# Reordering a mixer's output work and halving a Fourier product in a one-core Trainium2 layer

## The chip, the cores and the metric

One core of a Trainium2 chip runs one launch of the kernel. The metric is the device time of that launch in microseconds (us), as the median of several runs. A profile is one execution recorded by the hardware profiler; its span runs from the first to the last instruction. The engines are PE (TensorE, matrix products, with PEld for its weight loads), DVE (VectorE), ACT (ScalarE), POOL (GpSimd, which also issues some DMAs here) and SP (SyncE, which issues the weight DMAs). Each engine executes its own queue in order and waits on semaphores for the others.

## The reference

One layer of a diffusion backbone over 256 latent tokens with a prefix of 256 context tokens, 2048 channels, float32. Cut to what matters:

```
x, ctx = half SwiGLU FFN with norms, shift, scale, gate     (d_ff 5632, tokens 512)
q, k, v, beta, g, z, f = mixer_inputs(pre(x or ctx))        (one projection w_in, short conv)
o = gated delta rule, both directions, chunks of 64, 8 heads of 128, ctx state then latents
gd = rmsnorm(o, g_onorm) * silu(z)
ff = f.reshape(b, l, 8, 128)
fr = fft2(ff, axes=(positions, channels), norm='ortho').real
x  = post(x, concat([gd, fr]) @ w_out)
x  = half SwiGLU FFN again                                  (latent tokens only)
post(x, y): x + weight * mod_gate * rmsnorm(y, g_post)
```

The Fourier part of one group is real(W_t f W_c). With f real, it is cos_t (f cos_c) - sin_t (f sin_c), where cos_t and sin_t are 256 x 256 over positions. The cosine is symmetric and the sine antisymmetric under n -> 256 - n.

## The kernel before

All engines run hand-ordered queues; semaphores (`hs[...]` counts per head, from table `PER`) tie them. Weights stream through four raw slots by SP; ACT writes the high half of each and DVE the low half (`split_hi`, `split_lo`), and PE makes three products for each pair, so that float32 accuracy comes out of a faster format.

Stages in order of time: modulation rows and the first gate products; 11 FFN rounds over 512 tokens, in whose shadow DVE accumulates modulation rows (`mac`) that PE folds (`mod_reduce`, `transpose_mod`); norms; 20 pairs of projection tiles (`PROJ`) with convolution and gates; the mixer; the output projection; norms; 11 FFN rounds over 256 tokens; the end.

The mixer (`mixer_pe`, `mixer_dve`, `mixer_act`) runs one loop of ten passes, i from -1 to 8. A pass works on three heads at once: `a` is head i+1 (its chunk matrices are prepared), `m` is head i (its triangular systems are solved in five levels `y_level`/`x_level` on PE with `level_Y`, `level_S`, `level_T` on DVE; its Fourier group goes through `fnet_channels`, `fnet_mid`, `fnet_positions`, `fnet_out`, `fnet_hi`, `fnet_lo`), and `b` is head i-1 (its scan of eight steps `scan_read`, `scan_u`, `scan_write`, `scan_state`). `was` is head i-2: its normed and gated output (`out_root` and `out_hi` on ACT, `output` and `output_lo` on DVE) is written in this pass. Text below calls the pass with i = n "head n".

PE's order in a pass: `decay_sums(a)`, `products_k(a)`, `scan_write(b, 0)`, `y_level(m, 0)`, `scan_read(b, 1)`, `token_k(m, 0)`, `x_level(m, 0)`, and so on through five levels, with `fnet_positions(m)` after the fifth `x_level`, then `solve_w`, `out_sums(b)` and `solve_v`. DVE's order at the start of a pass: `chunk_half(a)`, `scan_state(b, 0)`, `chunk_matrix(a)`, `output(was)`, `output_lo(was)`, `level_Y(m, 0)`, `scan_u(b, 1)`, two `token_k`, `level_S(m, 0)`. PE's `x_level(m, 0)` waits for `level_Y(m, 0)`. POOL makes `strict_b` for a head as soon as the `n_mat` of the one before it is done.

`fnet_positions` sums four products into bank `B_B`, each of 128x128 weights from `f_mid` and 256 columns from the constants `dft_t` (cosine and sine, two halves of positions). In float32 one such product is two PE instructions. DVE copies the result to `f_out`, ACT writes its high part and DVE its low part to `xn2`.

The gains of the post norms lie across partitions in `post_g` (128 x 16) and are needed as rows on every partition. `gain_out` on POOL writes them element by element to DRAM (`gain_rows`, four rows: gain 0 for context, and gains 0, 1 and 2 for the latents), and `gain_in` reads a row back as a broadcast of 1 MB. The coefficients come from `coefs(r)` on DVE.

## Time and profile before

| | |
|---|---|
| three timed runs | 3143.86, 3140.58, 3143.63 us, median 3143.63 |
| profiled execution | 3139.69 us, span 3137.9 us |
| mean granted PE clock | 0.983 of 2.4 GHz |
| PE busy | 3018.2 us, 96% of the span |
| DVE, ACT, POOL busy | 1801.8, 965.7, 22.6 us |
| mixer, 1945 to 2265 us | PE busy 295.0 of 320 us |

Busy time is the time in which an engine has an instruction under way. Durations of PE instructions overlap (the end of a matmul is modelled), so for PE the distance from the start of one group to the start of the next is read. A bracket behind an instruction in a timeline gives the idle time of its engine before it and whose instruction ended it.

### The profile page before, as it was taken

What the parts mean: (1) busy time and instruction counts of PE and PEld (TensorE: products, weight loads), DVE (VectorE), ACT (ScalarE), POOL (GpSimd) and SP (SyncE); (2) the same over time, 40 slices, a digit from 0 to 9 for tenths busy, and PEclk for the clock granted to TensorE, in tenths of its full rate; (3) what the DMA queues carried; (4) which work ended last, traced back from release to release, by engine and by line L of the source; (5) the groups of instructions that cost most, each with busy time, mean ns of one, the idle gap of its engine ahead of it and who ended that gap; (6) DMA issues with size and microseconds to landing.
All of it is one profiled execution on the core that took longest, in us unless ns stands there. A gap on an engine that the chain in (4) does not pass through costs nothing. (4 is left out here: it accounts for less than half of the span.)

```text
span 3137.9 us, 44120 instructions
## 1 busy us (share of the span) xinstructions
PE 3018.2 (96%) x18262; PEld 2492.7 (79%) x18262; DVE 1801.8 (57%) x1977; ACT 965.7 (31%) x1211; POOL 22.6 (1%) x27
## 2 busy tenths in 40 slices
PE   5899999999999999998979999999998999999998
PEld 3588888888888888887868898777777888888887
DVE  3337565675555656555665464666655665565666
ACT  3222222222212122221343345222234433343433
POOL 0000000000000000000000000000000000000000
PEclk9999999999999999999989999999999999999999
DMA  8835444454544657567723353000154555555554
GB/s 316 294 104 189 146 162 148 152 196 136 171 151 148 247 189 274 198 217 177 287 63 94 108 164 105 2 2 2 64 171 143 183 192 187 187 183 191 182 193 135
DMA packets 305077, 506.05 MB, mean 161 GB/s; under 512 B 8253, under 2 KB 227909, under 8 KB 289061
## 3 DMA queue, kind: packets, MB, share of 16 engines
q1 hardware_dynamic: 302624, 494.73, 47.3%
q0 software_dynamic: 1472, 8.85, 0.8%
q8 instruction: 117, 1.92, 0.3%
q10 hardware_dynamic: 836, 0.33, 0.0%
q14 instruction: 28, 0.22, 0.0%
HBM read 501.75 MB, written 2.13 MB: 161 GB/s over the span
## 5 line engine op out<-in xcount | busy, mean ns | idle before, releaser
L1959 PE MATMUL ps<-xn,parts 128*128 128x512 f32 (+1 forms) x9008 | 1796.2, 361 | 16.4 <-DVE parts L1311 13.8
L1959 PEld LDWEIGHTS ps<-xn,parts 128*128 128x128 f32 x9008 | 1521.5, 189 | 290.1 <-issue 18.3
L1311 DVE TENSOR_TENSOR parts<-raw,parts 128x1024 fp32r<-128x1024 f32 x642 | 767.7, 1221 | 448.8 <-ACT parts L751 448.5
L751 ACT ACTIVATE parts<-raw 128x1024 fp32r<-128x1024 f32 x642 | 664.1, 1055 | 1114.6 <-PE ps L1959 889.6
L1959 PE MATMUL ps<-parts,h_parts 128*128 128x512 f32 x3168 | 729.5, 390 | 1.6 <-DVE h_f L1339 1.5
L1959 PEld LDWEIGHTS ps<-parts,h_parts 128*128 128x128 f32 x3168 | 591.5, 188 | 135.2 <-issue 6.1
L1327 DVE SCALAR_TENSOR_TENSOR macc<-raw,cs,macc 128x2048 f32<-128x2048 f32 x150 | 348.1, 2346 | 0.0
L1421 DVE TENSOR_TENSOR acc<-acc,ps 128x512 f32<-128x512 f32 x160 | 110.0, 687 | 212.4 <-PE ps L1959 212.4
L774 ACT ACTIVATE h_parts<-h_f 128x512 fp32r<-128x512 f32 (+1 forms) x42 | 35.1, 837 | 351.6 <-DVE h_f L1386 351.6
L1386 DVE TENSOR_TENSOR h_f<-silu_g,ps 128x1024 f32<-128x1024 f32 x20 | 24.4, 1222 | 140.5 <-PE ps L1959 140.5
L1959 PE MATMUL ps<-parts,xn 128*128 128x512 f32 x384 | 91.7, 394 | 0.0
L1959 PEld LDWEIGHTS ps<-parts,xn 128*128 128x128 f32 x384 | 71.0, 188 | 15.1 <-issue 0.5
L1413 DVE TENSOR_TENSOR acc<-acc,ps 128x1024 f32<-128x1024 f32 x44 | 53.7, 1221 | 39.1 <-PE ps L1959 36.1
L1380 DVE TENSOR_REDUCE h_f<-ps 128x512 f32<-128x1024 f32 x22 | 27.0, 1226 | 73.3 <-PE ps L1959 73.3
L1374 DVE TENSOR_REDUCE silu_g<-ps 128x512 f32<-128x1024 f32 x22 | 27.0, 1226 | 72.3 <-PE ps L1959 72.3
L1599 DVE SCALAR_TENSOR_TENSOR cv<-ps,convT,cv 128x248 f32<-128x248 f32 (+3 forms) x160 | 66.1, 471 | 0.0
L1681 PE MATMUL ps<-g_S,g_Y 64*64 64x64 f32 x1280 | 48.6, 228 | 14.6 <-DVE g_Y L1101 13.8
L1388 DVE TENSOR_TENSOR h_parts<-h_f,h_parts 128x512 fp32r<-128x512 f32 (+1 forms) x42 | 39.8, 946 | 37.9 <-ACT h_parts L774 37.9
L1681 PEld LDWEIGHTS ps<-g_S,g_Y 64*64 64x64 f32 x1280 | 43.1, 142 | 20.2 <-DVE g_Y L1101 16.4
L1959 PE MATMUL ps<-raw,cpad 128*32 128x512 f32 x256 | 40.7, 722 | 15.4 <-DMA raw<-in_w_mod 14.0
L1681 PE MATMUL ps<-g_T,n_T 64*64 64x64 f32 x1280 | 48.4, 228 | 2.3 <-DVE g_T L1107 2.1
L1681 PEld LDWEIGHTS ps<-g_T,n_T 64*64 64x64 f32 x1280 | 42.8, 141 | 7.9 <-DVE g_T L1107 3.8
(220 smaller groups left out, 1257.1 us busy)
## 6 DMA issues: line engine op xcount, KB each, us to landing
raw<-in_w_mod SPq DMA_DIRECT2D x144, 1024.0 KB, 5.4
raw<-in_w_gate SPq DMA_DIRECT2D x88, 1024.0 KB, 5.1
raw<-in_w_up SPq DMA_DIRECT2D x88, 1024.0 KB, 5.1
raw<-in_w_down SPq DMA_DIRECT2D x88, 1024.0 KB, 5.1
raw<-in_w_in SPq DMA_DIRECT2D x41, 1024.0 KB, 5.3
raw<-in_w_out SPq DMA_DIRECT2D x16, 1024.0 KB, 5.1
gr<-gain_rows POOLq DMA_DIRECT2D x3, 1024.0 KB, 7.6
x_in<-in_ctx SPq DMA_DIRECT2D x2, 1024.0 KB, 6.8
```

Of the source, the lines that this page charges most:

```text
L751: nc.scalar.activation(parts[:, unit % PART_SLOTS, 0, :], raw[:, slot, b * UNIT:(b + 1) * UNIT], ACT.Copy).then_inc(hi_ready, 1)
L774: nc.scalar.activation(gpart[:, 0, 2 * s:2 * s + 2, :], h_f32[:, :, 0:N], ACT.Copy).then_inc(h_hi, 1)
L1311: nc.vector.tensor_tensor(parts[:, pslot, 1, :], raw[:, slot, b * UNIT:(b + 1) * UNIT], parts[:, pslot, 0, :].bitcast(F32), ALU.subtract)\
L1327: ins = nc.vector.scalar_tensor_tensor(macc[:, s, :], raw[:, slot, :], cs[:, k, s:s + 1], macc[:, s, :], ALU.mult, ALU.add)
L1374: nc.vector.tensor_reduce(silu_g[:, :, 0:N], halves(4 * s), axis=mybir.AxisListType.X, op=ALU.add).then_inc(g_sum, 1)
L1380: nc.vector.tensor_reduce(h_f32[:, :, 0:N], halves(up), axis=mybir.AxisListType.X, op=ALU.add).then_inc(u_sum, 1)
L1388: nc.vector.tensor_tensor(gpart[:, 1, 2 * s:2 * s + 2, :], h_f32[:, :, 0:N], gpart[:, 0, 2 * s:2 * s + 2, :].bitcast(F32), ALU.subtract)\
L1413: nc.vector.tensor_tensor(a[:, :, cols], a[:, :, cols], ps[:, bank:bank + 2, :], ALU.add).then_inc(down_added, 1)
L1421: nc.vector.tensor_tensor(a[:, t, cols], a[:, t, cols], ps[:, down_bank(tiles, j, t), :], ALU.add).then_inc(down_added, 1)
L1599: nc.vector.scalar_tensor_tensor(o, s_, tap, o, ALU.mult, ALU.add).then_inc(conv_op, 1)
L1681: return nc.tensor.matmul(o, lhsT, rhs, start=start, stop=stop)
L1959: return nc.tensor.matmul(o, lhsT, rhs, start=start, stop=stop)
```

## The change

The post gains: `post_g` now holds two vectors at a time side by side; PE transposes them to 32 x 128 (`post_rows`), ACT copies them to `row_sb` (`post_row`), and POOL writes each pair with one DMA of 32 runs of 512 bytes. The second pair (gains 1 and 2 of the latents) is made right after the first norms. `coefs` becomes `post_coefs` and `pre_coefs`.

The mixer: `output` becomes `output_root` and `output_gate`. DVE runs `level_Y(m, 0)` and `scan_u(b, 1)` first, then `output_root`; `output_gate` comes after `scan_state(b, 3)` and `output_lo` after `scan_u(b, 5)`. ACT's `out_hi` moves from behind `out_root` to behind `transposed`. The last pass keeps its order.

The Fourier positions: cosine and sine products go to separate halves of bank `B_B` and are made for positions 0 to 128 alone, 129 columns. ACT copies the cosine sum to `f_mid` (`fnet_even`); DVE adds the sine sum for positions 0 to 128, and subtracts it, both read in reverse, for 129 to 255. `fnet_mid` waits for DVE's reads of the head before.

```diff
         cs = sb("cs", [P, KT, 2], R_LATE + 2048)
+        row_sb = sb("row_sb", [32, P], R_LATE + 2304)
         pick = sb("pick", [P, 2, 32], R_LATE + 3072)
...
         row_out, gr_ok = sem("row_out"), sem("gr_ok")
+        post_ok, row_T, row_ok = sem("post_ok"), sem("row_T"), sem("row_ok")
         coef_ok, y_scaled, ln_ok, acc3_zero = sem("coef_ok"), sem("y_scaled"), sem("ln_ok"), sem("acc3_zero")
...
             "kT": 2, "kd_ok": 2, "kbg_ok": 2, "vT": 2, "vb_ok": 8, "gam_mm": 1, "gam_exp": 1, "qg_ok": 1, "dT_mm": 1,
-            "dT_exp": 1, "qk_mm": 1, "p_half": 1, "p_ok": 3, "f_a": 1, "f_mid_ok": 1, "f_b": 1, "f_v": 1, "f_hi": 1,
+            "dT_exp": 1, "qk_mm": 1, "p_half": 1, "p_ok": 3, "f_a": 1, "f_mid_ok": 1, "f_b": 1, "f_even": 1, "f_v": 2, "f_hi": 1,
             "f_lo": 1,
...
-            def gain_out(n, s, coefs_done):
-
-                pool.wait_ge(coef_ok, coefs_done)
-                pool.dma_start(gain_rows[n].rearrange("(k p) -> p k", p=P), post_g[:, s, :],
-                               allow_slow_non_contiguous=True).then_inc(row_out, 16)
+            def gain_out(pair):
+
+                pool.wait_ge(row_ok, pair + 1)
+                pool.dma_start(gain_rows[2 * pair:2 * pair + 2].rearrange("n (k p) -> (n k) p", p=P), row_sb[:])\
+                    .then_inc(row_out, 16)
...
-                pool.wait_ge(row_out, 16 * max(2, n + 1))
+                pool.wait_ge(row_out, 16 * (n // 2 + 1))
                 pool.dma_start(dst, gain_rows[n:n + 1, :].to_broadcast([P, D])).then_inc(gr_ok, 16)
-            gain_out(0, 0, 4)
-            gain_out(1, 1, 4)
+            gain_out(0)
             pool.wait_ge(units_done, PART_SLOTS + 2 * S_KV.weight - 8)
...
+            gain_out(1)
             pool.wait_ge(mod_ok, 16)
...
                 strict_beta(Head(pool, h))
-            gain_out(2, 1, 6)
             pool.wait_ge(hs["qk_mm"], HEADS)
...
             nc.gpsimd.memset(acc3[:], 0.0).then_inc(acc3_zero, 1)
-            gain_out(3, 1, 7)
             gain_in(3, gr[:, 0, :])
...
                 m.wait("f_a")
-                m.last("f_b")
+                m.last("f_v")
                 nc.scalar.activation(flat(f_mid[:]), ps[:, B_A, :], ACT.Copy).then_inc(hs["f_mid_ok"], 1)
+
+            def fnet_even(m):
+                m.wait("f_b")
+                nc.scalar.activation(f_mid[:, 0, 0:P + 1], ps[:, B_B, 0:P + 1], ACT.Copy).then_inc(hs["f_even"], 1)
...
                     out_root(was)
-                    out_hi(was)
                 if m:
...
                     transposed(a)
+                if was:
+                    out_hi(was)
                 if m:
...
                 if m:
+                    fnet_even(m)
                     fnet_hi(m)
...
+
+            def post_row(pair):
+
+                act.wait_ge(row_T, pair + 1)
+                if pair:
+                    act.wait_ge(row_out, 16 * pair)
+                nc.scalar.activation(row_sb[:], ps[0:32, 7, 0:P], ACT.Copy).then_inc(row_ok, 1)
...
                             nc.scalar.preload_act_table_set("natural_log_exp_and_others")
+                    if sums is not None and sums[0] == 0 and u == 5:
+                        post_row(0)
                     if row is not None and u == 20:
...
                         split_hi(seg, i, u // 2 + 1, u % 2)
+                    if (n, uu) == (2, 1):
+                        post_row(1)
                     if (n, uu) in ((8, 1), (8, 3), (9, 2), (11, 1)):
...
                 dve.wait_ge(A["abT"], 1)
+                dve.wait_ge(row_out, 32)
                 for n in range(2):
...
             def fnet_out(m):
-                m.wait("f_b")
+                m.wait("f_even")
                 m.last("f_hi")
-                nc.vector.tensor_copy(f_out[:], ps[:, B_B, 0:SEQ]).then_inc(hs["f_v"], 1)
+                nc.vector.tensor_tensor(f_out[:, 0:P + 1], f_mid[:, 0, 0:P + 1], ps[:, B_B, SEQ:SEQ + P + 1],
+                                        ALU.add).then_inc(hs["f_v"], 1)
+                nc.vector.tensor_tensor(f_out[:, P + 1:SEQ], f_mid[:, 0, P - 1:0:-1],
+                                        ps[:, B_B, SEQ + P - 1:SEQ:-1], ALU.subtract).then_inc(hs["f_v"], 1)
...
-            def output(b):
+            def output_root(b):
                 b.wait("oss_inv")
...
+
+            def output_gate(b):
                 b.wait("o_n1")
...
                     scan_state(b, 0)
-                    output(was)
+                    output_root(was)
+                    output_gate(was)
                     output_lo(was)
...
                         split_out(s + 2)
-                    output(b)
+                    output_root(b)
+                    output_gate(b)
                     output_lo(b)
...
                     continue
+                level_Y(m, 0)
+                if b:
+                    scan_u(b, 1)
                 if was:
-                    output(was)
-                    output_lo(was)
-
-                level_Y(m, 0)
-                if b:
-                    scan_u(b, 1)
+                    output_root(was)
                 token_k(m, 0, 0)
...
                     scan_state(b, 3)
+                if was:
+                    output_gate(was)
...
                     scan_u(b, 5)
+                if was:
+                    output_lo(was)
...
-            def coefs(r):
-
-                for s in range(1 if r else 0, 2):
-                    nc.vector.scalar_tensor_tensor(post_g[:, s, :], modT[:, 3 * r + 2, s, :], (0.5, 1.0, 0.5)[r],
-                                                   vecT[:, V_GPOST + r, :], ALU.mult, ALU.mult).then_inc(coef_ok, 1)
-                    if r < 2:
-                        nc.vector.scalar_tensor_tensor(pre_a[:, s, :], modT[:, 3 * r + 4, s, :], 1.0,
-                                                       vecT[:, V_GPRE + r + 1, :], ALU.add, ALU.mult).then_inc(coef_ok, 1)
+            def post_coefs(at, r, s):
+
+                nc.vector.scalar_tensor_tensor(post_g[:, at, :], modT[:, 3 * r + 2, s, :], (0.5, 1.0, 0.5)[r],
+                                               vecT[:, V_GPOST + r, :], ALU.mult, ALU.mult).then_inc(post_ok, 1)
+
+            def pre_coefs(r, s):
+
+                nc.vector.scalar_tensor_tensor(pre_a[:, s, :], modT[:, 3 * r + 1, s, :], 1.0,
+                                               vecT[:, V_GPRE + r, :], ALU.add, ALU.mult).then_inc(coef_ok, 1)
...
                 ffn_round(S_A2, i, i + 7, TOK, h_parts, acc, i + 5, per=2)
-            coefs(0)
+            for s in range(2):
+                post_coefs(s, 0, s)
+                pre_coefs(1, s)
             ffn_round(S_A2, S_A2.iters - 1, ROUNDS - 1, TOK, h_parts, acc, S_A2.iters + 4, per=2, rows=0)
...
             norms(0, 4, acc, x_again, xn, lambda b: split_lo(S_KV, 0, 1, b))
+            dve.wait_ge(row_T, 1)
+            for at in range(2):
+                post_coefs(at, at + 1, 1)
...
-            coefs(1)
+            pre_coefs(2, 1)
             mixer_dve(dve, lambda n: split_lo(*out_unit(n)))
...
                 ffn_round(S_F2, i, i + ROUNDS, SEQ, h2_parts, acc3)
-            coefs(2)
             ffn_round(S_F2L, 0, 2 * ROUNDS - 1, SEQ, h2_parts, acc3, last=True, rows=2)
...
                 m.wait("p_half")
-                for n, (f, t) in enumerate(((0, 0), (0, 1), (1, 0), (1, 1))):
-                    last = mm(ps[:, B_B, 0:SEQ], f_mid[:, t, P * f:P * f + P], dft_t[:, f, t, :], n == 0, n == 3)
+                for f in range(2):
+                    for t in range(2):
+                        last = mm(ps[:, B_B, SEQ * f:SEQ * f + P + 1], f_mid[:, t, P * f:P * f + P],
+                                  dft_t[:, f, t, 0:P + 1], t == 0, t == 1)
                 inc(last, "f_b")
...
-            def ffn_round(seg, i, G, N, a, hp, mods=None, row=None, j0=0, both=False, follow=None):
+            def post_rows(pair):
+
+                pe.wait_ge(post_ok, 2 * pair + 2)
+                nc.tensor.transpose(ps[0:32, 7, 0:P], post_g[:].rearrange("p s k -> p (s k)"), ident).then_inc(row_T, 1)
+
+            def ffn_round(seg, i, G, N, a, hp, mods=None, row=None, j0=0, both=False, follow=None, post=False):
                 for j in range(8):
+                    if post and j == 2:
+                        pe.wait_ge(mod_copied, row + 6)
+                        post_rows(0)
                     s = j // 4
...
                     if j == 0 and row is not None:
+                        if post:
+                            pe.wait_ge(row_ok, 1)
                         mod_reduce(seg, i, row, both)
...
                 ffn_round(S_A2, i, i + 7, TOK, xn, h_parts, i + 12, i + 5)
-            ffn_round(S_A2, S_A2.iters - 1, ROUNDS - 1, TOK, xn, h_parts, S_A2.iters + 11, S_A2.iters + 4)
+            ffn_round(S_A2, S_A2.iters - 1, ROUNDS - 1, TOK, xn, h_parts, S_A2.iters + 11, S_A2.iters + 4,
+                      post=True)
...
                     wide_unit(seg, i, 2 * pr + uu // 2, uu % 2, (bank, bank + 1), N, a)
+                    if (n, uu) == (1, 3):
+                        post_rows(1)
                     if (n, uu) == (10, 1):
...
                     if (n, uu) == (11, 0):
```

## Rows read from the trace of the kernel before

**Rows 1.** The page's engine table: busy us, share of the span, instructions.

```profile
PE 3018.2 (96%) x18262; PEld 2492.7 (79%) x18262; DVE 1801.8 (57%) x1977; ACT 965.7 (31%) x1211; POOL 22.6 (1%) x27
```

**Rows 2.** Windows, the mixer: length, busy us of PE, PEld, DVE, ACT, POOL, clock, DMA.

```profile
1945.00:2265.00 320.00, 295.03 (x4846) 238.14 (x4844) 197.45 (x413) 75.56 (x176) 9.70 (x10) 0.95 0.03 10
```

**Rows 3.** Windows from one f_mid copy to the next, heads 1, 3 and 5.

```profile
1981.20:2017.70 36.50, 35.69 (x614) 28.75 (x616) 23.76 (x52) 7.71 (x19) 1.04 (x1) 1.00 0.01 2
...
2058.80:2099.90 41.10, 39.01 (x620) 31.75 (x622) 25.41 (x55) 9.35 (x23) 1.04 (x1) 0.92 0.01 2
...
2140.90:2181.20 40.30, 36.92 (x620) 29.58 (x622) 25.11 (x55) 9.34 (x23) 2.20 (x2) 1.00 0.03 2
```

**Rows 4.** Waits of PE, 2020 to 2240 us: us in total, times, longest.

```profile
PE ps L1681 <- DVE g_Y L1101: 10.5, 6, 2.1
PE ps L1681 <- issue: 0.8, 1, 0.8
```

**Rows 5.** Timeline of DVE, head 3: start us, length us.

```profile
2070.57 0.48 DVE L1174 SCALAR_TENSOR_TENSOR o_out<-ps,onorm,r_o 128x256 f32<-128x256 f32 x1
2071.08 0.97 DVE L1177 TENSOR_TENSOR o_out<-o_out,qzf 128x256 f32<-128x256 f32 x1
...
2072.87 0.68 DVE L1101 TENSOR_TENSOR g_Y<-ps,c 128x512 f32<-128x512 f32 x1
...
2085.06 0.69 DVE L1101 TENSOR_TENSOR g_Y<-ps,c 128x512 f32<-128x512 f32 x1 [0.47 <-PE ps L1681]
...
2091.71 0.69 DVE L1101 TENSOR_TENSOR g_Y<-ps,c 128x512 f32<-128x512 f32 x1 [0.53 <-PE ps L1681]
...
2100.96 0.69 DVE L1116 TENSOR_TENSOR g_S<-g_S,ps 128x512 f32<-128x512 f32 x1 [1.06 <-PE ps L1681]
```

**Rows 6.** Timeline of POOL.

```profile
2070.73 1.04 POOL L588 TENSOR_TENSOR strict_b<-early,sc_all 128x512 f32<-128x512 f32 x1 [40.09 <-DVE n_mat L1073]
...
2153.82 1.22 POOL L562 DMA_DIRECT2D gain_rows<-post_g  x1
```

**Rows 7.** Timeline of PE: x_level(0) and query_decays of heads 1, 3 and 6.

```profile
1993.27 1.15 PE L1681 MATMUL ps<-g_S,g_Y 64*64 64x64 f32 x32
...
1998.25 0.68 PE L1681 MATMUL ps<-early,gm 64*64 64x64 f32 x16
...
2073.61 1.97 PE L1681 MATMUL ps<-g_S,g_Y 64*64 64x64 f32 x32 [2.09 <-DVE g_Y L1101]
...
2080.45 0.68 PE L1681 MATMUL ps<-early,gm 64*64 64x64 f32 x16
...
2195.45 1.49 PE L1681 MATMUL ps<-g_S,g_Y 64*64 64x64 f32 x32 [1.54 <-DVE g_Y L1101]
...
2201.13 0.68 PE L1681 MATMUL ps<-early,gm 64*64 64x64 f32 x16
```

**Rows 8.** Windows, head 3 behind the wait; the clock is the third from last.

```profile
2074.00:2076.00 2.00, 2.00 (x34) 1.88 (x31) 1.32 (x3) 0.00 (x0) 0.00 (x0) 0.50 0.00 0
```

**Rows 9.** Timeline of DVE, head 1, where no output is.

```profile
1992.97 0.28 DVE L1156 TENSOR_TENSOR u_buf<-vt,ps 128x128 f32<-128x128 f32 x1
1993.38 0.69 DVE L1093 TENSOR_TENSOR kd<-ps,sc_all 128x512 f32<-128x512 f32 x1
```

**Rows 10.** The gate's product by its line: duration min/median/max in ns.

```profile
L1177 DVE TENSOR_TENSOR o_out<-o_out,qzf x8: 424/699/973, 2029.9 to 2300.9; 128x256 f32<-128x256 f32 x8
```

**Rows 11.** Timeline of PE: the position products of head 3 and what follows.

```profile
2101.34 1.95 PE L1681 MATMUL ps<-c,f_mid 128*128 128x256 f32 x8
2103.22 2.00 PE L1681 MATMUL ps<-g_S,kbg 64*128 64x64 f32 x32
```

**Rows 12.** Lines of PEld by form, 2059 to 2100 us: busy us, mean ns.

```profile
L1681 PEld LDWEIGHTS ps<-masks,sc_all 128*128 128x128 f32 x8 | 1.0, 190 | 0.0
```

**Rows 13.** Timeline of ACT, heads 2 and 3.

```profile
2081.18 0.38 ACT L654 ACTIVATE dT<-ps 128x256 f32<-128x256 f32 x1 [8.68 <-PE ps L1681]
...
2105.27 1.08 ACT L670 ACTIVATE wT<-ps 128x512 f32<-128x512 f32 x2 [1.07 <-PE ps L1681]
```

More of the change, by code:

```diff
@@ L1224, in mixer_dve @@
                     continue
-                if was:
-                    output(was)
-                    output_lo(was)
                 level_Y(m, 0)
@@ L1264, in mixer_dve @@
                     scan_u(b, 5)
+                if was:
+                    output_lo(was)
                 level_Y(m, 3)
```

## The prediction

> **What bounds the kernel now.** I read the page's engine table first: TensorE (PE) is busy for 3018 of 3138 us [rows 1], so nearly any time that leaves must come out of PE's own queue, either as work that PE no longer does, as idle time, or as time at the lower clock. The gain rows, their transposes and copies lie in stretches where PE is filled with weight products; the rest of the change lies in the mixer. I therefore took the mixer stage by itself: from 1945 to 2265 us PE is busy 295 of 320 us, VectorE (DVE) 197, ScalarE (ACT) 76 [rows 2]. PE is the bound there too, with 25 us of holes and a mean clock of 0.95.
>
> Next I cut the stage at each head's `f_mid` copy [rows 3]. A pass of the loop takes 36.5 us for head 1 and 41.1 us for head 3, with a mean clock of 1.00 and 0.92. The passes of heads 2 and 4 (41.1 and 41.0 us, 0.92) are the same but for 0.1 us; head 5 takes 40.3 at 1.00. Head 1's pass has the same loop body except that no `was` exists yet: it has no `output(was)`. The list of waits over heads 2 to 7 says what the hole is: PE waits for DVE's `g_Y` six times, 10.5 us in total, at most 2.1 us at once, and once for 0.8 us for nothing that the profile shows [rows 4].
>
> The timeline of DVE at head 3 names what DVE did meanwhile [rows 5]: after `n_mat` it runs `output`, 0.48 us for the first product and 0.97 for the second, then the low part once ACT has written the high one, and only at 2072.87 `level_Y`, for whose result PE has been waiting since 2071.5. POOL's `strict_b` lies from 2070.73 to 2071.77, on top of the 0.97 us product [rows 6].
>
> The hole costs more than itself. In PE's timeline `x_level(0)` starts at 2073.61 after 2.09 us idle, and the next landmark, `query_decays` (ps<-early,gm), at 2080.45: 6.84 us. In head 1 the same stretch runs from 1993.27 to 1998.25: 4.98 us, though it holds three small waits [rows 7]. The granted clock in that stretch of head 3 is 0.50, 1.2 GHz of 2.4 [rows 8]. So the lower clock adds 1.86 us to head 3 and, by the clock column and equal passes, to heads 2 and 4. At head 6 the stretch takes 2195.45 to 2201.13, 5.68 us: 0.7 us more [rows 7]. At head 5 the clock stayed up [rows 3], at head 7 too.
>
> **The change, part by part.**
>
> 1. *`level_Y` and `scan_u(1)` ahead of the output of the head before.* The six waits for `g_Y` in heads 2 to 7 go: **10.5 us** [rows 4]. `y_mm` is there when `n_mat` is done (in head 1 PE goes from its `token_k` straight into `x_level`), so nothing else is late in this place. I take the lower clock to go with the idle stretch that preceded it: 3 x 1.86 + 0.7 = **6.3 us**. Head 1, with small waits only, kept 1.00, and that is what the new passes should look like.
>
> 2. *Where the three pieces of the output go.* `output_root` (0.48 us, about 0.42 from start to start) now stands behind `scan_u(1)`. In head 1 `scan_u` starts at 1992.97, takes 0.28 us and `kd` follows at 1993.38 [rows 9]: of the root's 0.42 only 0.1 to 0.2 falls into a hole that was there. Behind it DVE is packed until `level_Y(1)`, and PE waits for its results. So 0.2 to 0.35 us of each root comes through; I take 0.3 for heads 2 to 6 and 0.1 for head 7, whose DVE starts this stretch early: **-1.6 us** (bounds 0 and -2.5). `output_gate` goes behind `scan_state(3)`, in front of a DVE wait of 0.47 us for PE; `output_lo` goes behind `scan_u(5)`, in front of one of 0.53 us [rows 5]. Each needs 0.42 (the product of the gate took 0.42 at least and 0.97 at most over the heads [rows 10]; 0.97 beside POOL, which is not at work there). Both fit: nothing. If POOL's kind of delay came back, the gate would cost 0.97 - 0.47 = 0.5 us a head, 3 us in all. ACT's `out_hi` moves behind `transposed`, into ACT's wait for PE's next token tile, and nothing of ACT's queue is late; nothing. PE's `scan_read(4)` waits for `o_n1`, which the root gives ten microseconds ahead.
>
> 3. *Fourier positions: four products of 129 columns for four of 256.* Each is two PE instructions. The eight take from 2101.34 to the start of the next group at 2103.22: 1.88 us, 235 ns each [rows 11]. The trace holds products with the same 128x128 f32 weights and 128 columns (gamma_rows): their eight loads take 1.0 us together, though each lasts 190 ns [rows 12], so they overlap and the pace is some 125 ns. With 129 columns that is 1.0 us. From above, the nearest row is the duration of a load: if eight such stood end to end the group would take 1.52 us and the change would bring 0.36 a head. But the row shows loads of just this size overlapping, so I take 0.88 us a head, 8 heads: **7.0 us** (bounds 2.9 and 7.1). The Trainium skill speaks against narrowing moving columns: "TensorE: Matmul & The Clock Gate", section on LDWEIGHTS, says that a load goes by the stationary operand's columns, which stay at 128 here, at about 107 ns; by that estimate eight need 0.85 us, less than the row's, and the sum would stay as it is.
>
>    What stands behind it must follow 0.88 us sooner. `solve_w` would start near 2102.4 and needs `s_ok`, which DVE's `level_S(4)` gives about 2101.65 [rows 5]: there. The new relay: ACT copies 129 columns (256 take 0.38 [rows 13], so about 0.28) from 2102.45 to 2102.75; DVE adds and subtracts in two instructions of some 0.28, start to start 0.2, to 2103.3; ACT's `fnet_hi` to 2103.75. ACT is next wanted for `wT`, which starts at 2105.27 now and takes 1.08 [rows 13] and at 2104.4 then. It has 0.65 us to spare, and PE has other work (`out_sums`, `solve_v(0)`, 1.6 us) before it needs the finished `wT`: another 0.5. No row shows a DVE read that walks backwards; bounds are 0.28 and the same stretched as the slowest product here was (0.97 for 0.42), 0.65. Both are covered. Uncovered they would cost what they exceed 1.1 us by.
>
> 4. *Gain rows.* Removed: four element-wise writes, of which one was issued in head 5 at 2153.82 [rows 6]; the 0.8 us in which PE waits for nothing shown lie 8 us behind it and nowhere else in the stage. I take them as that write's doing, which is a guess from the place alone: **0.8 us** (bounds 0 and 0.8). Added: two transposes on PE in streams without holes. Each is one instruction of 128 columns, 0.12 us at the pace of [rows 12]; I charge 0.15, **-0.3 us**. The two ACT copies of 32x128 and the `post_coefs` lie on engines that PE's stream covers (ACT is busy a third of the time). One less small DVE product in front of the first `gm`, for which PE waits: 0.1. SP's queue is not touched. POOL's queue now holds `gain_out(1)` behind a wait for ACT's row, with the masks' load behind it; that load then starts near 1650 instead of 1572 and is first needed near 1840: covered. The last 1 MB broadcast moves from 3071 to about 2371, where the DMA queues stand at a share of nearly 0. DVE's wait for `row_out` is over by then.
>
> Sum: 10.5 + 6.3 - 1.6 + 7.0 + 0.8 - 0.3 + 0.1 = **22.8 us**. The profiled execution took 3139.7 us (span 3137.9), so its like would take 3116.9. The median of the three timed runs is 3143.6, 3.9 above the profiled one; with the same loss it becomes **3120.8**.
>
> **Rivals.**
>
> - *The clock still falls.* The new passes keep waits of 0.2 to 0.5 us close together, and head 5 (2.09 us idle, clock up) against head 6 (1.54 us idle, clock down) shows that the length of the hole alone doesn't decide. Then the 6.3 us stay: gain 16.5, 3127.1. For it: that irregularity. Against it: head 1 and head 7, which have just such small waits, at 1.00. 12%.
> - *The weight loads set the pace of the narrow products.* Gain 0.36 a head: total 18.7, 3124.9. Against it the eight loads in 1.0 us. The rule of the Trainium skill cited above would, if its load time did not overlap at all with the products, give this direction. 12%.
> - *The stalls only move.* Gate or low part run long at their new place or the root's delay is passed on at every level, about 1.5 us a head more: gain 14, 3130. Against: the DVE waits at both places. 6%.
> - *Slower: the relay.* ACT's queue now holds `fnet_even`, a wait for PE, in front of `fnet_hi`, which waits for DVE, in front of `wT`, `vt` and the next head's `d_mat`. Every microsecond beyond 1.1 us of spare comes through in all eight heads. To be 0.2% slower (6.3 us) it must eat 22.8 and 6.3, 3.6 us a head, so the two DVE reads would have to take 4.7 us longer than I think, ten times their rows. Time then 3150. 3%.
>
> **How the numbers follow.** The forecast has 65%; 2% go to larger gains than the bounds allow. About 0.2%, 6.3 us, is what can be told from no change. Every case but the last is faster by more than that, though mixtures of the rivals could come near it: faster 0.94, same 0.03, slower 0.03. The range: from a full gain without the root's cost (25 us) and runs as low as the lowest of before (3 us under the median), some 3114, to the clock rival with a narrow part of the weights one, some 3130.
>
> **What would show it.** In the profile after: passes of heads 2 to 6 near 36.5 us or less at a clock of 1.00; no wait of PE for `g_Y` over 0.5 us in them; eight narrow products in 1.0 us; the `vt` and `wT` waits of PE unchanged; no 0.8 us wait in head 5; four small writes replaced by two. The prediction would be wrong if the clock row still shows 0.50 behind `x_level(0)`, or if PE waits for `wT` in every head.

## The result and the profile after

The changed kernel takes 3103.65 us in the median of four runs (3100.97 to 3104.17), the one before in the same session 3142.11 (3134.81 to 3143.86). The ratio is 0.988 (0.9863 to 0.9897): 38 us faster, where I had forecast 22.8 and at most 30. It was measured a second time beside the best version: 3100.78 us against 3136.83, 0.989 (0.9874 to 0.9907), which is 36 us by the medians.

The page's engine table after, to [rows 1] (PE is busy 20 us less in a span of 3101.9, 36 us shorter; the other 16 us were idle time):

```profile
PE 2998.3 (97%) x18264; PEld 2478.4 (80%) x18264; DVE 1798.1 (58%) x1985; ACT 968.3 (31%) x1221; POOL 18.5 (1%) x25
```

Windows from one `f_mid` copy to the next after, heads 1 to 7, to [rows 3]:

```profile
1970.30:2005.90 35.60, 34.78 (x612) 28.21 (x614) 23.76 (x53) 7.96 (x19) 1.04 (x1) 1.00 0.01 2
2005.90:2042.30 36.40, 35.67 (x618) 28.99 (x620) 24.42 (x56) 9.62 (x23) 1.04 (x1) 1.00 0.01 2
...
2115.10:2151.50 36.40, 35.67 (x619) 28.98 (x621) 24.42 (x56) 9.62 (x24) 1.05 (x1) 1.00 0.01 2
...
2187.90:2222.50 34.60, 32.60 (x552) 26.60 (x552) 20.99 (x49) 8.41 (x21) 0.58 (x1) 1.00 0.08 28
sum 252.20, PE 245.75 PEld 199.72 DVE 166.26 ACT 64.47 POOL 5.80; mean PE 35.11 PEld 28.53 DVE 23.75 ACT 9.21 POOL 0.83
```

Heads 2 to 6 take 36.4 us each at a clock of 1.00; before they took 39.3 to 41.1. The seven passes take 252.2 us against 275.5 (36.5 + 41.1 + 41.1 + 41.0 + 40.3 + 39.3 + 36.2).

PE's timeline after, head 3, to [rows 7] and [rows 11]: `x_level(0)` follows `token_k` without a wait, three small waits come behind it, and the narrow products take 1.04 us from start to start (2080.17 to 2081.21).

```profile
2053.75 0.44 PE L1713 MATMUL ps<-c,kv 128*64 128x128 f32 x4
2054.12 1.15 PE L1713 MATMUL ps<-g_S,g_Y 64*64 64x64 f32 x32
...
2056.86 0.44 PE L1713 MATMUL ps<-st,wT 128*64 128x128 f32 x4 [0.33 <-DVE st L1188]
2057.49 1.15 PE L1713 MATMUL ps<-g_T,n_T 64*64 64x64 f32 x32 [0.18 <-DVE g_T L1125]
2058.85 0.49 PE L1713 MATMUL ps<-u_buf,kd 64*128 64x128 f32 x4 [0.22 <-DVE u_buf L1177]
2059.28 0.68 PE L1713 MATMUL ps<-early,gm 64*64 64x64 f32 x16
...
2080.17 1.11 PE L1713 MATMUL ps<-c,f_mid 128*128 128x129 f32 x8
2081.21 2.00 PE L1713 MATMUL ps<-g_S,kbg 64*128 64x64 f32 x32
```

DVE's timeline after, head 3, to [rows 5] and [rows 9]: the three pieces of the output and the Fourier relay. The gate takes 0.42 us at its new place and leaves `level_Y` a gap of 0.14; the reversed read of 127 columns takes no longer than the forward one.

```profile
2054.02 0.48 DVE L1195 SCALAR_TENSOR_TENSOR o_out<-ps,onorm,r_o 128x256 f32<-128x256 f32 x1
...
2063.33 0.42 DVE L1200 TENSOR_TENSOR o_out<-o_out,qzf 128x256 f32<-128x256 f32 x1
2063.89 0.69 DVE L1119 TENSOR_TENSOR g_Y<-ps,c 128x512 f32<-128x512 f32 x1
...
2069.92 0.42 DVE L1205 TENSOR_TENSOR xn<-o_out,xn 128x256 fp32r<-128x256 f32 x1
2070.53 0.69 DVE L1119 TENSOR_TENSOR g_Y<-ps,c 128x512 f32<-128x512 f32 x1 [0.19 <-PE ps L1713]
...
2081.63 0.29 DVE L1163 TENSOR_TENSOR f_out<-f_mid,ps 128x129 f32<-128x129 f32 x1 [1.15 <-ACT f_mid L663]
2081.83 0.28 DVE L1165 TENSOR_TENSOR f_out<-f_mid,ps 128x127 f32<-128x127 f32 x1
```

PE is busy 245.75 us in the seven passes where it was busy 260.83, and idle 6.5 us where it was idle 14.7. The waits for `g_Y` have gone, but small waits for `u_buf`, `st` and `g_T` take 5.4 us where they took 2.0.

So the mixer gave 23.2 us. The rest lies ahead of it. PE's timeline of the kernel *before*, in the last FFN round over 512 tokens, has a line that the prediction did not read:

```profile
1439.74 8.77 PE L1959 MATMUL ps<-xn,parts 128*128 128x512 f32 x38
1459.13 16.23 PE L1959 MATMUL ps<-xn,parts 128*128 128x512 f32 x64 [10.62 <-DVE parts L1311]
```

PE waits 10.6 us for a weight unit. The waits of all engines before, 1425 to 1470 us, name the chain: DVE waited for ACT, ACT for the load of `w_up`, 28.8 us for one of the two:

```profile
ACT parts L751 <- DMA raw<-in_w_up: 36.7, 2, 28.8
DVE parts L1311 <- ACT parts L751: 24.8, 2, 21.8
...
PE ps L1959 <- DVE parts L1311: 10.6, 1, 10.6
```

The same query after:

```profile
ACT parts L757 <- DMA raw<-in_w_up: 17.8, 2, 9.8
```

Windows before in that stretch (DMA share and GB/s are the last two columns) show what the DMA engines did meanwhile: from about 1434 to 1452 us they had packets under way and moved little. POOL had issued the two element-wise writes from 1428.3 on.

```profile
1432.00:1436.00 4.00, 4.00 (x19) 3.31 (x18) 3.98 (x3) 0.00 (x0) 0.00 (x0) 1.00 1.72 166
1436.00:1440.00 4.00, 4.00 (x20) 3.30 (x19) 0.00 (x0) 0.00 (x0) 0.00 (x0) 1.00 1.10 5
...
1444.00:1448.00 4.00, 4.00 (x19) 3.30 (x19) 0.00 (x0) 0.00 (x0) 0.00 (x0) 1.00 1.10 39
...
1452.00:1456.00 4.00, 0.00 (x0) 0.00 (x0) 0.00 (x0) 0.00 (x0) 0.00 (x0) 0.50 0.80 226
1456.00:1460.00 4.00, 0.87 (x2) 0.81 (x3) 2.24 (x2) 2.00 (x2) 0.00 (x0) 0.50 0.97 406
```

The load of `w_up` issued at 1432.60 took 24.0 us to land; in the changed kernel such a load takes 5.2. The packets under way were those of the weights themselves: from 1440 to 1448 us the weight queue has 250 packets that fill 86.5% of the engines' time, and no packet of the writes is on record. In the changed kernel the same 8 us hold 848 weight packets at 91.2%. So each weight packet took longer; what inside the DMA engines made it so, the trace does not show.

By landmarks, with the second profile of the changed kernel (span 3099.5, 38.4 us shorter): first `rdiag` product of the first norms 1587.2 to 1576.5, -10.6; from there to the first `f_mid` copy 394.1 to 390.8, -3.3; seven passes -23.25; the rest -1.2. The first profile had started 4 us late: PE waited 16.9 us there for the first modulation rows, in the other traces 13 to 15; what the remaining 2 us are is not known.

### The profile page after: what moved, and what is told of

Read it like the earlier page. It is cut to its first block and busy times, and to the rows that moved or that the text cites. A ratio compares the mean times of both kernels' runs of the same rounds, so it can differ in the third digit from the quotient of the medians.

```text
span 3101.9 us, 44143 instructions
## 1 busy us (share of the span) xinstructions
PE 2998.3 (97%) x18264; PEld 2478.4 (80%) x18264; DVE 1798.1 (58%) x1985; ACT 968.3 (31%) x1221; POOL 18.5 (1%) x25
## 5 line engine op out<-in xcount | busy, mean ns | idle before, releaser
L1440 DVE TENSOR_TENSOR acc<-acc,ps 128x1024 f32<-128x1024 f32 x44 | 53.7, 1222 | 39.1 <-PE ps L1993 36.1
L1993 PE MATMUL ps<-raw,cpad 128*32 128x512 f32 x256 | 38.7, 689 | 18.3 <-DMA raw<-in_w_mod 16.9
L1713 PE MATMUL ps<-g_T,n_T 64*64 64x64 f32 x1280 | 46.1, 222 | 2.9 <-DVE g_T L1125 2.8
```

What stands on the lines that cost most here:

```text
L1440: nc.vector.tensor_tensor(a[:, :, cols], a[:, :, cols], ps[:, bank:bank + 2, :], ALU.add).then_inc(down_added, 1)
L1713: return nc.tensor.matmul(o, lhsT, rhs, start=start, stop=stop)
L1993: return nc.tensor.matmul(o, lhsT, rhs, start=start, stop=stop)
```

## The experiments

Each ran beside the kernel before on the same chip. The kernel before took 3136 to 3138 us in these sessions, and its profiled execution of 3139.7 belongs to the slower half of its runs (3131.6 to 3141.6).

**The gain rows alone.** The kernel before with the parts of the diff that concern `gain_out`, `row_sb`, `post_rows`, `post_row`, `post_coefs` and `pre_coefs`:

```diff
-            gain_out(0, 0, 4)
-            gain_out(1, 1, 4)
+            gain_out(0)
...
-            gain_out(2, 1, 6)
...
-            gain_out(3, 1, 7)
```

> The kernel before with the gain rows alone changed (transposed on PE, written as 32 runs of 512 bytes, coefficients early); mixer and Fourier part as before. Theory A, element-wise writes delay the weight load issued behind them: the one PE wait of 10.6 us for `parts` near 1450 us goes, with the 1.6 us at the lower clock behind it, and the 0.8 us in head 5; two transposes cost 0.3: 12.7 us less than before, ratio 0.996. Theory B, that wait comes from the order of the loads and not from the writes: it stays, and the kernel is 0 to 1 us faster. The mixer keeps its holes of 2.1 us before `level_Y` in either case.

Measured: 3119.8 against 3137.7 us, ratio 0.9948 (0.9934 to 0.9962), 16 us (12 to 21). PE's longest wait for `parts` in the whole kernel is 2.0 us. Theory A holds and B falls. The gain is above A's 12.7, which lies near the low end of the interval. In the profile (19.9 us less) 11.4 lie ahead of `rdiag`, 3.7 between `rdiag` and the first `f_mid`, and 5.4 in the mixer; what follows takes 0.6 longer. There the holes of 2.1 us are all still there (13.8 us for `g_Y`, as before), but the clock fell less behind them:

```profile
2002.60:2041.70 39.10, 36.53 (x618) 29.40 (x618) 25.05 (x54) 9.31 (x22) 1.04 (x1) 1.00 0.01 2
2041.70:2081.80 40.10, 37.73 (x618) 30.59 (x620) 25.35 (x55) 9.34 (x22) 1.04 (x1) 0.96 0.01 2
```

That is head 2 at 39.1 us and 1.00, head 3 at 40.1 and 0.96, where the trace before had 41.1 and 0.92 for both. The lower clock behind a given hole is not a fixed price. Head 5, without a write, takes 39.2 us, where it took 40.3 with one.

**The order alone.** The kernel before with the mixer's order changed:

```diff
-                if was:
-                    output(was)
-                    output_lo(was)
-
                 level_Y(m, 0)
                 if b:
                     scan_u(b, 1)
+                if was:
+                    output_root(was)
```

> The kernel before with the order of the output work alone changed (root, gate, low part on DVE, out_hi on ACT). My prediction's terms: 10.5 us of idle time and 6.3 us at the lower clock go, 1.6 us of root come in: 15.2 us less, ratio 0.9952, heads 2 to 6 near 37.3 us each. Rival, the clock falls all the same: 9 us less. The 10.6 us wait near 1450 us stays under both.

Measured: 0.9974 (0.9963 to 0.9985), 8 us (5 to 12), half of the forecast. The forecast of 15.2 us lies outside the interval. Yet heads 2, 3, 4 and 6 take 37.23 us, the 37.3 that I expected. The profile shows one place of loss, head 5, at 45.9 us. PE's timeline there, after POOL's write of one gain row at 2146.24:

```profile
2153.06 0.68 PE L1688 MATMUL ps<-early,n_mat 64*64 64x64 f32 x15
2155.65 0.49 PE L1688 MATMUL ps<-early,n_mat 64*64 64x64 f32 x3 [1.91 <-issue]
2156.37 1.11 PE L1688 MATMUL ps<-early,n_mat 64*64 64x64 f32 x14 [0.23 <-issue]
2157.41 0.80 PE L1688 MATMUL ps<-u_buf,kd 64*128 64x128 f32 x4
2158.14 1.97 PE L1688 MATMUL ps<-g_T,n_T 64*64 64x64 f32 x32
```

PE stops in the middle of a group of products that wait for no semaphore, and runs at half speed (a group of 32 in 1.9 us instead of 1.08) until 2169.9. The element-wise write that stays in this kernel costs 8.7 us here; the kernel before paid about 1 us for it. This execution was the slowest of the seven (3134.8 us, 5 above the median), so in a typical run the write costs less than that, and part of the missing 7 us may be clock that a typical run of the kernel before does not lose.

**The Fourier positions alone,** with their relay on ACT and DVE.

```diff
-                for n, (f, t) in enumerate(((0, 0), (0, 1), (1, 0), (1, 1))):
-                    last = mm(ps[:, B_B, 0:SEQ], f_mid[:, t, P * f:P * f + P], dft_t[:, f, t, :], n == 0, n == 3)
+                for f in range(2):
+                    for t in range(2):
+                        last = mm(ps[:, B_B, SEQ * f:SEQ * f + P + 1], f_mid[:, t, P * f:P * f + P],
+                                  dft_t[:, f, t, 0:P + 1], t == 0, t == 1)
```

> The kernel before with the Fourier positions alone changed. Prediction's term: eight products in 1.0 us instead of 1.88, 0.88 us in each of eight heads, 7.0 us less, ratio 0.9978. Rival, weight loads set the pace: 1.5 us for the eight, 2.9 us less. The holes before `level_Y` and the wait near 1450 us stay.

Measured: 0.9978 (0.9969 to 0.9987), 6.9 us (4.1 to 9.7). Head 1 falls from 36.46 to 35.63 us: 0.83 a head, 6.6 in eight. The rival of the weight loads falls: its 2.9 us lie below the interval.

**The two writes apart.**

```diff
             gain_out(0, 0, 4)
+            pool.wait_ge(units_done, PART_SLOTS + 2 * S_KV.weight - 16)
             gain_out(1, 1, 4)
```

> The kernel before with its second element-wise write of 2048 runs held back by 8 weight units (about 44 us), so that the two no longer stand together; nothing else changed. Theory A1, each write delays the load behind it by its own length, and the raw slots cover one: the load waits some 13 us instead of 25, PE needs it 16 us after its issue, so PE's wait falls from 10.6 us to under 2 in all, 10 us less than before. Theory A2, writes cost PE their full length wherever they stand: two waits of some 5 us, time as before. Theory B (the writes are not the cause): one wait of 10.6 us as before.

Measured: 0.9983 (0.9974 to 0.9992), 5.3 us (2.5 to 8.2). PE now waits twice:

```profile
1451.78 43.77 PE L1960 MATMUL ps<-xn,parts 128*128 128x512 f32 x192 [1.71 <-DVE parts L1312]
1497.68 22.04 PE L1960 MATMUL ps<-xn,parts 128*128 128x512 f32 x96 [2.13 <-DVE parts L1312]
```

and the waits of ACT for `w_up` in this round show the dose, one write in flight instead of two:

```profile
ACT parts L752 <- DMA raw<-in_w_up: 49.8, 4, 19.9
```

The longest wait of ACT for a load is 10.1 us without such writes, 19.9 with one and 28.8 with two: 9.8 and 8.9 us for each, about what the last write took before POOL could read it back (9.8 us). With two, 18.7 us of delay made PE wait 10.6, so the raw slots had covered 8.1. With one, 9.8 less 8.1 leaves 1.7, and the first wait is 1.71. The other traces with two writes fit the same sum: in the order alone ACT waits 30.9 and PE 12.7, in the run with all but the gain rows 29.4 and 11.2. A1 is right in kind, and A2, two waits of 5 us and no gain, falls. A1's sum, under 2 us of waiting, was too small by the second wait, and the 10 us that it promised lie outside the interval; the timed gain of 5.3 is near the idle time saved (10.6 - 3.8 = 6.8).

**All but the gain rows.** The changed kernel with `gain_out` and `coefs` as before, the complement of the first experiment.

> The changed kernel with the gain rows as before (four element-wise writes, coefficients as before); mixer order and Fourier part as changed. Theory A, the writes delay the load behind them: the wait of 10.6 us near 1450 us is back, 12.2 us slower than the changed kernel; and if the write issued in head 5 causes the 0.8 us in which PE waits for nothing shown, that wait is back too, within 12 us of the write. Rival: the load's delay needs something else of the kernel before: as fast as the changed kernel within 1 us.

Measured: 3120.9 us, ratio 0.9952 (0.9935 to 0.9968), where the changed kernel has 0.988. PE's wait for `parts` is back at 11.2 us, and head 5, with the write, takes 39.4 us, against 36.4 for heads 2, 3, 4 and 6, with a wait of 1.4 us for nothing shown and the clock at 1.00 in that pass. I had expected 12.2 us more than the changed kernel. Taken last, the gain rows are thus worth 17 to 20 us by the medians (3120.9 less 3103.65 and less 3100.8); taken first, 16. The two kernels ran in different sessions; by their ratios to the kernel before the distance is 19 to 23 us.

**Only the low part late.** The kernel before with one call moved:

```diff
                 if was:
                     output(was)
-                    output_lo(was)
...
                 level_Y(m, 0)
                 if b:
                     scan_u(b, 1)
+                if was:
+                    output_lo(was)
```

> The kernel before with one call moved: `output_lo` behind `level_Y(m, 0)` and `scan_u(b, 1)`, while root and gate stay in front. The hole before `x_level(0)` shrinks from 2.09 us to about 1.2 (the wait for ACT's high part and the low part go). If the lower clock goes by the length of the hole, it stays up: 6 x 0.85 of idle and 6.3 of clock, 11 us less. If a hole of 1.2 us is enough at this place, the stretch behind it still shows 0.50 in several heads: 5 us less or even nothing more.

Measured: 0.999 (0.9981 to 1.0), 3 us (0 to 6), far from the 11 us of the first case and nearer the second. But it is the mechanism of the first that shows. The hole is 1.18 us, and the clock stays up behind it in every head without a write. Windows of heads 2, 3 and 5:

```profile
2019.60:2058.20 38.60, 36.59 (x620) 29.47 (x622) 25.02 (x55) 9.35 (x23) 1.04 (x1) 1.00 0.01 2
2058.20:2096.70 38.50, 36.49 (x618) 29.37 (x617) 24.91 (x55) 9.31 (x22) 1.04 (x1) 1.00 0.01 2
...
2135.30:2177.10 41.80, 38.40 (x620) 30.87 (x622) 25.16 (x55) 9.35 (x23) 2.20 (x2) 0.96 0.03 2
```

Head 5 with the write takes 3.2 us more than its neighbours. That a typical run of the kernel before loses less to the clock than its profile did (6.3 us) accounts for the rest in kind; the runs do not size it. The profile of this version is itself 6.9 us shorter than that of the kernel before.

**Four writes in the changed kernel.** On POOL, behind `strict_beta(Head(pool, h))`:

```diff
+                if 3 <= h < 7:
+                    pool.dma_start(spare_rows[h].rearrange("(k p) -> p k", p=P), post_g[:, 0, :],
+                                   allow_slow_non_contiguous=True).then_inc(spare_out, 16)
```

> The changed kernel with four added element-wise writes of one `post_g` vector (2048 runs of 4 bytes) to a spare DRAM tensor, one in each of the heads 2 to 5, right behind `strict_b`, where the kernel before had one; the output is the same. If such a write holds back PE's instruction stream, PE waits for nothing shown (0.8, 1.4 and 1.9 us in the three traces that have one write there) within 12 us of each, the clock may fall behind it, and the heads with a write take 36.4 + 1 to 9 us: 12 us slower than the changed kernel, with a wide spread. Rival, the wait in head 5 belongs to head 5 (its place in the instruction memory): heads 2 to 4 stay at 36.4.

Measured: 3126.9 us against 3100.8 for the changed kernel in the same session, 26 us slower, twice the 12 that I expected; one of its ten runs took 8113 us and is not explained. The writes fell into heads 1 to 4, one earlier than I wrote. These take 41.3, 46.1, 42.5 and 43.1 us, heads 5 and 6 without one 36.4. A write costs 5.7, 9.7, 6.1 and 6.7 us, and the rival, that the wait belongs to head 5, falls. PE's six waits for nothing shown all lie within 10 us of one; four of them:

```profile
2028.18 0.27 PE L1720 MATMUL ps<-early,n_mat 64*64 64x64 f32 x2 [0.54 <-issue]
2028.83 1.25 PE L1720 MATMUL ps<-early,n_mat 64*64 64x64 f32 x15 [0.38 <-issue]
...
2075.11 1.21 PE L1720 MATMUL ps<-early,n_mat 64*64 64x64 f32 x19 [1.74 <-issue]
...
2117.06 0.48 PE L1720 MATMUL ps<-early,n_mat 64*64 64x64 f32 x2 [1.20 <-issue]
```

The window behind the second of the four writes shows the lower clock, third column from last:

```profile
2030.00:2046.00 16.00, 15.63 (x144) 12.74 (x143) 8.08 (x18) 2.75 (x7) 0.00 (x0) 0.50 0.01 1
```

Over all runs, ten such writes were issued in the mixer. Behind nine of them PE stops for nothing shown, and the first stop begins 7.3 to 9.1 us after the issue, at different instructions. Behind the tenth, in the run with the Fourier positions alone, no such stop shows; there PE waited 2.08 us for `g_Y` right behind the issue, as in the kernel before, where the stop came all the same. The traces without a write in the mixer have no such stop. The price is not the same everywhere: 3.0 and 3.2 us in two of the runs above, and behind the last write of the kernel before (3059.95 us, in the last FFN rounds) PE is busy without a break up to 3080.

The DMA queues of that trace from 2010 to 2100 us show whose traffic shares the engines with the writes: ten packets of instructions, 16 KB each.

```profile
q0 software_dynamic: 96, 0.02, 2.2%
q8 instruction: 10, 0.16, 0.9%
```

That a fetch of instructions is what comes late is argued from this and from the waits that no semaphore explains; the trace does not show one fetch with its delay, and such packets come as often where no write is (8 in 60 us, from 2160 to 2220). The Trainium skill, "Advanced Engine Details and Errata", section on the ISA Cache, states lines of 16 KB, 256 instructions, for the engines; the packet size agrees.

**The root later, and the second `kbg` tile later.** Two versions of the changed kernel. The first moves one call:

```diff
-                if was:
-                    output_root(was)
                 token_k(m, 0, 0)
...
+                if was:
+                    output_root(was)
                 level_S(m, 1)
```

> The changed kernel with `output_root` moved from behind `scan_u(b, 1)` to in front of `level_S(m, 1)`, where DVE waits 0.94 us for PE. If the root's 0.4 us pushes PE's small waits in the first level (0.33 us for `st`, of which head 1 had 0.15), the waits fall by 0.2 to 0.3 us in each of six heads: 1.5 us less than the changed kernel. Rival: PE's sum of waits is set elsewhere, no change.

The second puts the root behind `level_T(m, 1)` and moves the tile too:

```diff
                 token_k(m, 1, 0)
+                if b:
+                    scan_u(b, 2)
+
+                level_Y(m, 1)
                 token_k(m, 1, 1)
-                if b:
-                    scan_u(b, 2)
-
-                level_Y(m, 1)
```

> The changed kernel with `output_root` behind `level_T(m, 1)` and the second `kbg` tile behind `level_Y(m, 1)` instead of in front. DVE's packed stretch of the first level gets 1.0 us shorter, so PE's waits for `st` (0.33) and `u_buf` (0.22) shrink or go, in seven heads: 3 us less than the changed kernel. Rival: `transposed` on PE then waits for the second `kbg` tile and gives it back.

Measured: 3099.5 us, ratio 0.9881 (0.9864 to 0.9897), and 3097.3 us, ratio 0.9881 (0.9865 to 0.9898). The passes of heads 2 to 6 fall from 36.40 to 36.23 and 35.95, so the root's first place had cost 0.17 us a head against its second, not 0.3, and the seven passes together fall by 0.85 of the 1.5 us expected. In the second version no wait of PE for a `kbg` tile has come in, and PE's wait for `u_buf` is gone from heads 2 to 6:

```profile
PE ps L1713 <- DVE g_T L1125: 0.9, 5, 0.2
PE ps L1713 <- DVE st L1188: 0.8, 5, 0.2
```

To set it beside the changed kernel, both ran once more in one session.

> The changed kernel once more, beside the next one on the same chip: 3103 us, ratio 0.988.

> The version with `output_root` behind `level_T(m, 1)` and the second `kbg` tile behind `level_Y(m, 1)` once more: heads 2 to 6 at 35.95 against 36.40 us and head 1 at 35.34 against 35.62, which makes 2.8 us less than the changed kernel over the mixer.

Measured: 3100.78 us (3100.24 to 3102.68), 0.989 (0.9874 to 0.9907), for the changed kernel and 3097.71 us (3096.38 to 3098.15), 0.9878 (0.9862 to 0.9895), for the second version, four runs each, with no value shared between them. Their ratios to the kernel before overlap; the seven passes, 252.25 and 249.42 us, agree with the 2.8 us expected. It is 3 us faster than the changed kernel and the best one of the study.

## Why the prediction was wrong

**The step that failed is part 4, the gain rows.** The sum, 22.8 us, is 15.7 short of the 38.5 measured by the medians. Part 4 sized the removed element-wise writes at 0.8 us with bounds of 0 and 0.8, and the opening says that the gain rows "lie in stretches where PE is filled with weight products". PE is filled there except for the longest wait of the round, 10.6 us, which begins 20 us after the two writes were issued. The list of PE's waits over the whole kernel, which I had, names it (DVE `parts`: 13.8 us in 3 waits, the longest 10.6). I gave a cause only to the waits of the mixer, and read the windows around the writes up to 1448 us, half a microsecond before the hole opens. The first experiment gives these writes 16 us (12 to 21), taken alone. In the profiles it is 10.6 us of waiting, 1.7 us of lower clock behind it (64 products take 16.23 us there, and 14.6 at full clock), 1 us in head 5, and some 3 us between `rdiag` and the first `f_mid`. That last piece is lower clock too: every trace without the two writes takes 390.4 to 391.6 us there, every one with them 393.1 to 394.1. Why the clock goes that way so regularly is open; between the kernel before and the first experiment the waits in that stretch differ by one of 0.8 us.

**Parts 1 and 2, the order.** Right in mechanism and, within the mixer, in size: the six waits went, the clock stayed at 1.00, and all seven passes gave 23.2 us, where the terms that fall between the first and the last `f_mid` (10.5, 6.3, -1.6, 0.8 and seven times 0.88) make 22.2. Part of that agreement is luck, since the 6.3 and the 10.5 are readings of one execution, and the order alone, timed, gave 8 us. The root cost 0.17 us a head, not 0.3. The 6.3 us of clock were read rightly from that execution but are no property of the kernel: the same holes cost less in the first experiment. A hole of 1.2 us left the clock up.

**The sum as a sum.** The parts were added as if each had its own price. The write in head 5 cost about 1 us while PE had a hole of 2.1 us in every pass, and 3.0 to 8.7 us where that hole was closed or smaller. The order alone is thus worth 8 us and not 15, and the gain rows more when they come last. The three parts taken alone give 16, 8 and 7 us, 31 in all, where the whole change gives 36 to 38.

**Part 3, the Fourier positions.** Right: 1.04 us for the eight products where I expected 1.0, 6.9 us timed for 7.0. The relay of ACT, DVE and ACT stayed hidden: `fnet_hi` starts at 2082.15 in head 3, before the solve's products are done, and PE waits nowhere for `wT` in heads 1 to 7 (0.3 us once in head 0, as before).

**The rest of part 4.** The two transposes and copies are not seen in any wait, and the load of `masks`, issued at 1646 us, makes PE wait nowhere. The rivals (clock, weight loads, stalls that move, relay) all failed. None was on the side where the error was: a cost of the kernel before that I had not seen. The low end of the range, 3114, is also 1 to 2 us lower than the gain of 25 and the 3 us given for it make; it was still 10 us too high.

## What to carry to other kernels

Before costing the removal of a DMA, look at every transfer and every wait within some 30 us behind each of its issues, and not only at who waits for the transfer itself: nobody waited for these writes, and they held up a weight load by 9 us each. Read the kernel's list of waits whole, its longest single waits above all, and attach a cause to each before any stage is cut out. A disturbance that a hole hides is not cheap: its price appears when the hole is closed, so changes of order and changes of transfers should be timed together as well as alone.

## What the runs showed of the hardware

A write of 8 KB to DRAM in 2048 runs of 4 bytes holds back a 1 MB load that is issued behind it on another queue: by 9.8 us with one write in flight, by 18.7 to 20.8 with two; the same data as 32 runs of 512 bytes (16 KB for two vectors) lands in 2.2 to 2.8 us and delays nothing that shows. The Trainium skill, "DMA: Bandwidth & Descriptors", section "Why small descriptors are slow (HBM only)", speaks of a fixed overhead for each packet and of fixed descriptor metadata for each DMA operation. The trace agrees in direction; by it, an estimate is 4.6 ns a run over all engines (the mean of the two delays, 9.35 us, by 2048).

Behind such a write in the mixer PE stops for 0.2 to 1.9 us at a time, waiting for no semaphore, in nine of ten cases. After these stops the granted clock was at 0.50 for 7 to 17 us in the run with four writes, which is the larger part of their price of 5.7 to 9.7 us each, and for 13 us in the run with the order alone. In the run with all but the gain rows it stayed at 1.00, and the write cost 3.0 us. That a fetch of instructions comes late is not shown.

DVE reads a source backwards (127 float32 columns, one operand in PSUM) in 0.28 us, the same as forwards.
